# Four chunks on the unnormalized input, sums and lower parts on VectorE, TensorE's layer loops written out

## What is computed

```python
def rms_norm(x, g):            # the factor 1/sqrt(mean(x*x) + eps) is one number per token
    return x * rsqrt(mean(x * x) + eps) * g
# per layer, cut:
x = x + 0.5 * (silu(h @ w_gate) * (h @ w_up)) @ w_down      # h = rms_norm(x, ffn1_norm)
proj = rms_norm(x, mix_norm) @ w_in                          # q, k, v, pooling input, gates
x = x + merge(pooling, attention) @ w_out
x = x + 0.5 * (silu(h @ w_gate) * (h @ w_up)) @ w_down      # h = rms_norm(x, ffn2_norm)
```

## Time and profile before

| | |
|---|---|
| median of three runs | 2128.6 us (2124.53 to 2132.08) |
| profiled execution | 2127.77 us |
| its span, first to last instruction | 2126.0 us |
| mean granted TensorE clock | 0.989 |
| TensorE, VectorE, ScalarE, GpSimd busy | 97%, 61%, 51%, 15% |

### The profile page before, as it was taken

The page is one execution under the profiler, slowest core; times in us unless marked ns, Lnnn a source line. Parts: engine busy times, 40 slices in busy tenths (PEclk is TensorE's granted clock), DMA queues, the critical chain, the costliest instruction groups (busy, mean ns, idle before and its releaser), DMA issues.

```text
span 2126.0 us, 36714 instructions
## 1 busy us (share of the span) xinstructions
PE 2063.8 (97%) x14600; PEld 1917.8 (90%) x14600; DVE 1298.3 (61%) x1472; ACT 1087.7 (51%) x1312; POOL 316.8 (15%) x239
## 2 busy tenths in 40 slices
PE   6999999999999999999999999999998999999997
PEld 5999989899889999898999899999997989999996
DVE  6555655655665566467556645567775545567775
ACT  5445555544554465545446443356655443355554
POOL 3000331300010033033004003230004103220001
PEclk9999999999999999999999999999998999999998
DMA  6554534454455454345555434544543434544451
GB/s 244 196 178 178 179 127 152 161 193 179 159 189 187 178 179 170 128 159 203 188 184 184 147 139 147 191 180 177 192 178 132 162 134 145 183 162 176 182 193 60
DMA packets 53287, 360.04 MB, mean 169 GB/s; under 512 B 6321, under 2 KB 7729, under 8 KB 10545
## 3 DMA queue, kind: packets, MB, share of 16 engines
q1 hardware_dynamic: 49248, 350.01, 45.9%
q10 hardware_dynamic: 3328, 4.20, 0.7%
q0 software_dynamic: 592, 4.19, 0.5%
HBM read 353.14 MB, written 1.05 MB: 167 GB/s over the span
## 4 chain that ended last, share of the span: by engine, by line
PE 60%; issue 30%; POOL 5%; ACT 2%; DVE 2%; DMA 1%; SPq 0%; POOLq 0%; DVEq 0%; ACTq 0%
PE up_two L1394 7%; PE gate_two L1359 7%; PE gate_two L1360 7%; PE gate_two L1361 7%; PE gate_two L1394 6%; PE bank L1359 5%; PE bank L1361 5%; PE bank L1360 5%; PE up_two L1396 4%; PE gate_two L1396 3%; POOL br_parts L405 2%; POOL in_parts L405 2%; PE bank L1468 1%; PE up_two L1482 1%; PE up_two L1498 1%
## 5 line engine op out<-in xcount | busy, mean ns | idle before, releaser
L921 DVE TENSOR_TENSOR w_lo<-raw,w_hi 128x2048 fp32r<-128x2048 f32 x330 | 767.1, 2325 | 345.5 <-ACT w_hi L545 345.3
L545 ACT ACTIVATE w_hi<-raw 128x2048 fp32r<-128x2048 f32 x330 | 628.3, 1904 | 72.8 <-PE bank L1361 68.7
L1360 PE MATMUL bank<-hid_hi,w_lo 128*128 128x256 f32 x960 | 271.6, 283 | 0.0
L1359 PE MATMUL bank<-hid_lo,w_hi 128*128 128x256 f32 x960 | 271.5, 283 | 0.0
L1361 PE MATMUL bank<-hid_hi,w_hi 128*128 128x256 f32 x960 | 271.5, 283 | 0.0
L1394 PE MATMUL gate_two<-in_parts,w_hi 128*128 128x512 f32 x640 | 229.1, 400 | 6.6 <-POOL in_parts L405 6.6
L1359 PE MATMUL gate_two<-br_parts,w_hi 128*128 128x256 f32 x768 | 223.8, 291 | 11.6 <-POOL br_parts L405 5.7
L1394 PE MATMUL up_two<-in_parts,w_hi 128*128 128x512 f32 x640 | 227.8, 399 | 0.4 <-DVE w_lo L921 0.4
L1360 PE MATMUL gate_two<-br_parts,w_lo 128*128 128x256 f32 x768 | 219.7, 286 | 0.0
L1361 PE MATMUL gate_two<-br_parts,w_hi 128*128 128x256 f32 x768 | 219.7, 286 | 0.0
L1359 PEld LDWEIGHTS bank<-hid_lo,w_hi 128*128 128x128 f32 x960 | 183.8, 191 | 3.0
(11 more groups left out here) (257 smaller groups left out, 4517.5 us busy)
## 6 DMA issues: line engine op xcount, KB each, us to landing
raw<-stream SPq DMA_DIRECT2D x330, 1024.0 KB, 4.8
area<-rpb POOLq DMA_DIRECT2D x2, 1536.0 KB, 7.7
softT<-area ACTq DMA_DIRECT2D x32, 64.0 KB, 4.4
konst<-consts SPq DMA_DIRECT2D x1, 1344.0 KB, 13.4
x<-xT SPq DMA_DIRECT2D x4, 256.0 KB, 4.0
area<-area ACTq DMA_DIRECT2D x8, 128.0 KB, 4.9
ret_turn<-area ACTq DMA_DIRECT2D x8, 128.0 KB, 4.7
result<-x SPq DMA_DIRECT2D x4, 256.0 KB, 2.0
```

The costliest lines, as they stand in the source:

```text
L545: act.activation(w_hi[:, s, :], raw[:, s, :], ACT.Copy).then_inc(hi_ready[s], 1)
L921: dve.tensor_tensor(w_lo[:, s, :], raw[:, s, :], w_hi[:, s, :].bitcast(F32), ALU.subtract).then_inc(lo_ready[s], 1)
L1359: pe.matmul(out, whi, xlo, start=start, stop=False, skip_group_check=True)
L1360: pe.matmul(out, wlo, xhi, start=False, stop=False, skip_group_check=True)
```

## The change

1. In the first block's FFNs four chunks instead of two (A0, B0, A1, B1) use `br_parts`; A2 is the first that uses `in_parts`, and waits for all eight lower parts. The mean is taken after the second chunk, the factor is spread in the middle of the third.
2. Pair 1 of the FFN is multiplied twice with the factor too, as pair 0. D0 waits for the last of these multiplications. Silu of pair 0, its product and its split move to the head of the third step, silu of pair 1 and the eight upper parts to the head of the fourth step on ScalarE; the eight lower parts are made at the end of VectorE's fifth step.
3. In the mixer the first six chunks use `br_parts`; the two value chunks get the factor when ScalarE takes them out (two 128x256 operations for one 128x512), the seventh chunk waits for all lower parts. The floor under k's variance is scaled likewise (`k_floor`).
4. The sums of squares, the lower parts of the first block's norms and those of the merged branches in both blocks go from GpSimd to VectorE.
5. TensorE's two layer loops become Python loops, so that its list is written out for both layers; the loops inside an FFN stay.

The diff, cut:

```diff
@@ GpSimd
                 power(rs[:, :], ms[:, :]).then_inc(rs_ready.sem, 1)
-                for k in range(DT):
-                    pool.wait_ge(xn_hi.sem, here.at(xn_hi, DT * n + k + 1))
-                    rest(in_lo[:, k, :], work_of[n][:, k, :], in_hi[:, k, :]).then_inc(xn_ready.sem, 1)
...
-                sum_squares(here, 0)
                 norm(here, 0)
-                sum_squares(here, 1)
                 norm(here, 1)
@@ ScalarE, FFN step
+                    if c == c0 + 2:
+                        act.wait_ge(gate_scaled.sem, here.at(gate_scaled, 4 * f + 1))
+                        act.activation(glu_a, glu_a, ACT.Silu).then_inc(gate_act.sem, 1)
+                        hidden_upper(here, f * PAIRS)
+                    if c == c0 + 3:
+                        act.wait_ge(gate_scaled.sem, here.at(gate_scaled, 4 * f + 3))
+                        act.activation(glu_a, glu_a, ACT.Silu).then_inc(gate_act.sem, 1)
+                        norm_upper(here, 2 * f)
                     if c != final:
                         chunk_done(here, c, turn)
...
                     if c == c0 + 1:
-                        hidden_upper(here, f * PAIRS)
+                        norm_mean(here, 2 * f)
@@ VectorE, FFN step
+                    if c == c0:
+                        sum_squares(here, 2 * f)
+                    if c == c0 + 2:
+                        norm_factor(here, 2 * f)
+                        times_factor(0, 1, gate_sum, f * PAIRS + 1)
+                        norm(here, 2 * f, gains)
+                        times_factor(0, 2, gate_act, f * PAIRS + 1)
+                        dve.wait_ge(gate_scaled.sem, here.at(gate_scaled, 4 * f + 2))
+                        product(0)
+                        hidden_lower(here, f * PAIRS)
                     if c != final:
                         chunk_done(here, c, turn)
...
+                    if c == c0 + 2:
+                        times_factor(1, 1, gate_sum, f * PAIRS + 2)
...
+                    if c == c0 + 3:
+                        times_factor(1, 2, gate_act, f * PAIRS + 2)
+                        dve.wait_ge(gate_scaled.sem, here.at(gate_scaled, 4 * f + 4))
+                        dve.wait_ge(hid_ready.sem, here.at(hid_ready, f * PAIRS + 1))
+                        product(1)
...
+                    if c == c0 + 4:
+                        hidden_lower(here, f * PAIRS + 1)
+                        split_after(here, c, turn)
+                        norm_lower(here, 2 * f)
+                        return
@@ VectorE, mixer
                     if m == 0:
+                        split_after(here, c)
+                        sum_squares(here, 1)
+                    if m == 2:
+                        split_after(here, c)
                         norm_factor(here, 1)
                         norm(here, 1, cur[:, C_MIX:C_MIX + DT])
-                        split_after(here, c)
...
+                            if j >= 1:
+                                merged_lower(here, j - 1, merged1, in_hi, in_lo)
+                        merged_lower(here, HALVES - 1, merged1, in_hi, in_lo)
...
+                    if m == 4:
+                        norm_lower(here, 1)
@@ TensorE
                     if kind == "D":
                         pe.wait_ge(hid_ready.sem, here.at(hid_ready, i + (f * PAIRS + 1)))
+                        if c == c0 + 4 and here.kind == 0:
+                            pe.wait_ge(gate_scaled.sem, here.at(gate_scaled, 4 * f + 4))
...
-                    elif not (c0 <= c < c0 + 3 and start(c)):
+                    elif not (c0 <= c < c0 + 4 and start(c)):
+                        if c == c0 + 5 and here.kind == 0:
+                            pe.wait_ge(xn_ready.sem, here.at(xn_ready, DT * (2 * f + 1)))
...
-            with pe.Fori(0, DEPTH) as layer:
+            for layer in range(DEPTH):
...
-                    if m < 3:
+                    if m == 6:
+                        pe.wait_ge(xn_ready.sem, here.at(xn_ready, 2 * DT))
+                    if m < 4:
                         norm_start(1, FFN_CHUNKS)(c)
                     elif m in (4, 5):
-                        tokens(c, bank, in_hi, in_lo)
+                        tokens(c, bank, br_hi, br_lo)
```

More of the change, by code:

```diff
@@ L410, in norm @@
                 power(rs[:, :], ms[:, :]).then_inc(rs_ready.sem, 1)
-                for k in range(DT):
-                    pool.wait_ge(xn_hi.sem, here.at(xn_hi, DT * n + k + 1))
-                    rest(in_lo[:, k, :], work_of[n][:, k, :], in_hi[:, k, :]).then_inc(xn_ready.sem, 1)
-            def merged_lower(here, merged, upper, lower):
-                for j in range(HALVES):
-                    pool.wait_ge(merged_hi.sem, here.at(merged_hi, j + 1))
-                    rest(lower[:, 2 * j:2 * j + 2, :], merged[:, 2 * j:2 * j + 2, :], upper[:, 2 * j:2 * j + 2, :]
-                         ).then_inc(merged_lo.sem, 1)
             def layer_norm(here, n):
@@ L434, in layer_norm @@
                     rest(br_lo[:, k, :], x[:, k, :], br_hi[:, k, :]).then_inc(xs_ready.sem, 1)
-            def sum_squares(here, n):
-                first = work_of[n][:, 0:2, :]
-                for j in range(1, HALVES):
-                    pool.wait_ge(sq_ready.sem, here.at(sq_ready, HALVES * (n - 1) + j + 1))
-                    if j >= 2:
-                        pool.wait_ge(sq_sum.sem, here.at(sq_sum, (HALVES - 1) * n + j - 1))
-                    pool.tensor_tensor(first, first, work_of[n][:, 2 * j:2 * j + 2, :], ALU.add).then_inc(sq_sum.sem, 1)
             with pool.Fori(0, DEPTH) as layer:
                 here = Place(0, layer)
-                sum_squares(here, 0)
                 norm(here, 0)
-                sum_squares(here, 1)
                 norm(here, 1)
@@ L483, in _ @@
                                        ).then_inc(pool_d.sem, 1)
-                merged_lower(here, merged1, in_hi, in_lo)
-                sum_squares(here, 2)
                 norm(here, 2)
@@ L680, in _ @@
                     bank = banks[4 + m % 2]
-                    if m == 0:
-                        norm_mean(here, 1)
                     if m < 4:
@@ L690, in _ @@
                     elif m < 6:
-                        act.activation(v_tok[:, :, (m - 4) * T:(m - 3) * T], bank[:, :, :], ACT.Copy
-                                       ).then_inc(mix_evac.sem, 1)
+                        if m == 4:
+                            act.wait_ge(rs_ready.sem, here.at(rs_ready, 2))
+                        for a in range(TT):
+                            e = act.activation(v_tok[:, a, (m - 4) * T:(m - 3) * T], bank[:, a, :], ACT.Copy,
+                                               scale=rs[:, a:a + 1])
+                        e.then_inc(mix_evac.sem, 1)
                     elif m < 8:
@@ L708, in _ @@
                         split_after(here, c)
-                        norm_upper(here, 1)
+                    if m == 1:
+                        norm_mean(here, 1)
                     if 1 <= m < 5:
@@ L739, in _ @@
                         split_after(here, c)
+                    if m == 3:
+                        norm_upper(here, 1)
                     if m in (15, 16):
@@ L950, in norm, with sum_squares, norm_lower, merged_lower @@
                                              in1=rstd_norms[n], op0=ALU.mult, op1=ALU.mult).then_inc(xnf_ready.sem, 1)
+            def sum_squares(here, n):
+                first = work_of[n][:, 0:2, :]
+                for j in range(1, HALVES):
+                    dve.wait_ge(sq_ready.sem, here.at(sq_ready, HALVES * (n - 1) + j + 1))
+                    if j >= 2:
+                        dve.wait_ge(sq_sum.sem, here.at(sq_sum, (HALVES - 1) * n + j - 1))
+                    dve.tensor_tensor(first, first, work_of[n][:, 2 * j:2 * j + 2, :], ALU.add).then_inc(sq_sum.sem, 1)
+            def norm_lower(here, n):
+                for k in range(DT):
+                    dve.wait_ge(xn_hi.sem, here.at(xn_hi, DT * n + k + 1))
+                    rest(in_lo[:, k, :], work_of[n][:, k, :], in_hi[:, k, :]).then_inc(xn_ready.sem, 1)
+            def merged_lower(here, j, merged, upper, lower):
+                dve.wait_ge(merged_hi.sem, here.at(merged_hi, j + 1))
+                rest(lower[:, 2 * j:2 * j + 2, :], merged[:, 2 * j:2 * j + 2, :], upper[:, 2 * j:2 * j + 2, :]
+                     ).then_inc(merged_lo.sem, 1)
             def add_upper(out, pair):
@@ L1260, in _ @@
                                           ).then_inc(merged_ready.sem, 1)
+                        if j >= 1:
+                            merged_lower(here, j - 1, merged2, br_hi, br_lo)
+                        if j == HALVES - 1:
+                            merged_lower(here, j, merged2, br_hi, br_lo)
                     if 32 <= m < 36:
```

94 lines of the change are left out of this document (40 added, 54 removed).

## The result

The changed kernel takes 2190.8 us (median of four runs, 2187.7 to 2194.8), the kernel before 2128.8 beside it: a ratio of 1.0294 (95% interval 1.0266 to 1.0321), slower by 62 us. The prediction was 2187.0, range 2150 to 2212. The profiled execution has a span of 2186.5 at a mean granted clock of 0.974; before it was 2126.0 at 0.989.

A forecast was written before the change was run, and what follows sets the result against it. TensorE, busy 97% of the span, bounds the kernel, so only waits and clock count. FFN starts +37.4, mixer +6.2, merged input -2.0, loops -1.6 and clock +19.2 gave +59.2 on 2127.77: 2187.0 us, range 2150 to 2212.

The forecast's parts named there:

- The sixth chunk's wait: In every FFN start TensorE waits 7.8 us for VectorE's eight lower parts, which come after D0's end.
- D0's wait: First down chunk of each FFN starts 6.3 us after TensorE was free, awaiting the last multiplication with the factor.
- The fourth FFN start: Second layer's second FFN, first to sixth chunk: 44.0 us against 35.33 before, +8.7.
- The other three: First to sixth chunk in the first three FFNs: +8.8, +9.0 and +10.9 us; all four together +37.4.
- The mixer: Mixer's six chunks take 46.2 us in both layers, with waits for the mean and at the seventh chunk; +6.2.
- The merged input: Its lower parts move from GpSimd to VectorE, so 1.0 us of TensorE's wait goes in both layers: -2.0.
- The loops: Written out, they remove 2.45 us at the first layer's end (already counted in 10.9) and 1.6 at the second block's.
- The clock: TensorE's low clock behind eight new long waits, 2.4 us each: +19.2; bounds 13.6 and 24.4, or nothing.
- The range: 2158 (clock free, FFN starts 2 us shorter each) to 2212; 2150 to 2212 to hold 8 in 10.
- Rival 1: In the FFN starts D0 doesn't wait and only the lower parts' wait remains: +24.3, 2152 us; chance 0.08.
- 3: Nothing measurable: new waits about a third, some 20 us, clock staying up, gain cancelling them: 2128 us; chance 0.04.
- Rival 2: Faster: FFN lower parts ready before the sixth chunk, factor 6.3 us earlier: -23.8, 2104 us; chance 0.06.

The follow-up runs named there:

- the run with the waits filled: Changed kernel with unused products (44 ahead of D0's wait, 62 behind D0) so TensorE doesn't stand still in its eight waits; 2172.9 us, ratio 1.0214.
- the last kernel: Changed kernel with four FFN edits (bank 3 wait, ScalarE's order, later tables, earlier lower parts), and the mixer's sums and lower parts moved ahead; 2102.3 us, ratio 0.9867.
- the run with the later tables: Changed kernel, but GpSimd loads the second block's tables only after the first block's last lower parts are made; 2189.6 us, ratio 1.0277.

## Why the prediction was right, step by step

The sign, the mechanism and the size were right. The sum gave +40.0 of waits and +19.2 of clock; the run with the waits filled puts 18 of the measured 62 on the clock and leaves 44. That the total came out within 4 us is in part luck: two errors of over 5 us in the FFN starts cancel (below).

- **The sixth chunk's wait**, 7.8 predicted, was 7.66 once and 7.79 three times, by the chain that was read off the old trace. The lower part that the trace did not show, bounded at 0.29 and 0.40 each, has a duration of 0.42 on VectorE and a pitch of 0.34 (2.77 for eight), against 2.7 taken.
- **D0's wait**, 6.3 predicted, was 5.6, with D0 at +29.7 instead of +30.4. The step that was wrong inside it is "queued ahead of everything, the eight upper parts, 2.55": VectorE's w_lo was as late to within 1.3 us, so that of two queues in parallel the second stood almost where the first did. The total came out near because only the later of the two counts.
- **The fourth FFN start** is the term that failed in size: 44.0 was predicted, and with the slow part of D0 (2.7) taken off 48.9 was measured. The step that failed is one the prediction did not make: it said of GpSimd what it no longer does, and not what it then does earlier. Freed of the norms, GpSimd came to the tables 8.6 us sooner in the FFN, and a collision that had cost a wait of 0.42 fell on the path to D0 (5.6).
- **The other three**, less the slow part of D0 (2.9, 2.2 and 2.6), were 44.3, 43.2 and 43.3 for 45.7, 44.0 and 45.7 (577.7 to 623.4). In the third the step "VectorE can't have its third w_lo before 588.0" was wrong: D0 starts at +29.74 as in the second, so ScalarE's loop did not hold VectorE up. Against the old lengths and the earlier start of the third the four give 7.4, 8.3, 8.4 and 13.5, together +37.7 for +37.4 predicted: 32.1, and 5.6 from the tables. The other three and the fourth without its tables are 5.3 us shorter than predicted, the tables 5.6 longer; the total hid both.
- **The mixer**, 46.2 predicted, took 46.52 twice, with waits of 1.70 and 1.68 (1.9 and 2.0 predicted) and a short slow stretch behind the first of them that was not in the sum.
- **The merged input**, -2.0: its wait is gone. No experiment separated it.
- **The loops**, 2.45 and -1.6: the first gap went, the second fell by 1.8. But the first gave nothing that lasted in the kernel before, since the next waits took it, and in the second block the changed kernel loses 3.1 us at half clock some 260 us behind the loop's end, at a place that the sum did not have.
- **The clock**, 2.4 for each long wait, was 2.2 by the runs. The price of 1.7 behind a wait of 2.2 came from one row: the wait of 2.23 at 949.97 was followed by half clock, the wait of 2.24 in the earlier trace rows was not (clock 1.00 in the earlier trace rows). So the lower bound of 13.6 was less sure than it looks.
- **The range**: 2187.0 less 19.2 and less four times 2 is 2159.8, not 2158; nothing hangs on it.
- **The rivals.** Rival 1 (D0 doesn't wait) and 3 did not come. Rival 2, 2104 us, named its deciding point as whether the lower parts run before D0's end. That is the order of two calls, and with it, the factor's wait, ScalarE's order, the tables and the mixer's lists mended the time is 2102.3. So the price of that rival was about right for a kernel in which none of the new waits stands. Its deciding point alone is not enough: with only the lower parts moved the time was 2151.6.

## What to carry to other kernels

When work moves to an engine with time to spare, its place in that engine's list can decide, and not the load, as it did here (VectorE was 61% busy): ask of each moved step what the engine waits for just ahead of it, and move the step in front of that wait. A consumer should wait only ahead of the first product that conflicts (here the fourth bank, 4.4 us into D0), and a freed engine's next job must be placed too, because it will start earlier and may hold up another engine. On TensorE a wait in the middle of a run of products cost its length and then some 2 us more, for products at the low clock.

## What the runs showed of the hardware

- **VectorE and GpSimd.** A 128x512 subtraction on VectorE that starts 0.85 us into GpSimd's 6.74 us multiplication lasts 6.43 us instead of 0.69, and ends about half a microsecond behind it. The Trainium skill, "SBUF — State Buffer", section Who interferes with whom, says that a VectorE instruction with two inputs in SBUF contends with a GpSimd instruction that reads SBUF, and calls the port pair that these two share an exclusive lock. The trace agrees, in this row, in that of the kernel before (6.50, where an addition with one input in up_two beside the same multiplication took 0.68), and in the last kernel (8.25 for a w_lo of 2.29).
- **The clock's steps.** Before the sixth chunk the clock falls to 0.50 inside the wait of 7.7 to 7.8 us, before the wait ends, and stays there for 6.8 us in the first, third and fourth FFN start and for 10.2 us in the second; with the same waits the run with the later tables had 10.2 us at all four. The sixth chunks lost between 1.3 us (6.96 for 5.65) and 2.9 (8.53 in that other run). The 2.2 us per wait is a mean over eight.
- **Short waits.** Waits of 1.68 to 1.70 us twice in each mixer were followed by 3.4 us at 0.50 once in each in the changed kernel, by 6.8 us in the run with the later tables, and by none in the second mixer of the kernel with the waits filled. The waits of 0.35 us and less in the last kernel's first block, and its one of 1.07, were followed by none.
